# Rotary exchange by on-chip transfers and gate maxima through device memory, in a three-layer hybrid block on one core

## The reference

```python
z = rms_norm(x, w) @ w_in + b_in
aq, ak = rope(z[AQ]), rope(z[AK])          # 8 heads of 64
ya = dilated_mixture_attention(aq, ak, z[AV])
mq, mk = silu(causal_short_conv(z[MQ:MV]))
hm = mlstm_chunkwise(mq, mk, z[MV], z[MI], z[MF])   # 4 heads of 128
x = x + (sigmoid(z[GA]) * (ya @ w_proj_att) + sigmoid(z[GB]) * (yb @ w_proj_mlstm)) @ w_out
x = x + square(relu(rms_norm(x) @ w_ff1)) @ w_ff2
```

```python
t1, t2 = t[..., :8], t[..., 8:16]
concatenate([t1 * cos - t2 * sin, t2 * cos + t1 * sin, t[..., 16:]])
```

## Time and profile before

| | |
|---|---|
| median of 3 runs | 2493.03 us (2492.36 to 2494.66) |
| the profiled execution's own time | 2492.54 us |
| its span, first to last instruction | 2490.7 us |
| PE busy | 2444.8 us (98%), granted clock 0.998 on the mean |
| DVE, ACT, POOL busy | 983.9, 868.4, 1099.4 us (40%, 35%, 44%) |
| transfers | 215.18 MB, 86 GB/s on the mean |

### The profile page before, as it was taken

The page is one execution under the profiler, slowest core; times in us unless marked ns, Lnnn a source line. Parts: engine busy times, 40 slices in busy tenths (PEclk is TensorE's granted clock), DMA queues, the critical chain, the costliest instruction groups (busy, mean ns, idle before and its releaser), DMA issues.

```text
span 2490.7 us, 30039 instructions
## 1 busy us (share of the span) xinstructions
PE 2444.8 (98%) x11732; PEld 1984.8 (80%) x11732; DVE 983.9 (40%) x1582; ACT 868.4 (35%) x1092; POOL 1099.4 (44%) x808
## 2 busy tenths in 40 slices
PE   7999999999999999999999999999999999999998
PEld 6777788888888867788888888898776688888887
DVE  4545553310202455554310212567695543322202
ACT  4355333421323345333421323442325323322213
POOL 3423344544544532345454544443342255555542
PEclk9999999999999999999999999999999999999999
DMA  4211223223222221222322322321222132232231
GB/s 140 90 63 53 83 85 101 85 102 101 85 102 89 85 68 51 85 78 91 101 101 85 101 102 70 101 77 51 74 85 68 55 101 92 95 101 85 101 101 68
DMA packets 174028, 215.18 MB, mean 86 GB/s; under 512 B 7652, under 2 KB 155044, under 8 KB 173924
## 3 DMA queue, kind: packets, MB, share of 16 engines
q1 hardware_dynamic: 171572, 210.39, 26.1%
q10 hardware_dynamic: 2352, 3.31, 0.4%
HBM read 211.20 MB, written 2.10 MB: 86 GB/s over the span
## 4 chain that ended last, share of the span: by engine, by line
issue 49%; POOL 31%; PE 19%; DMA 0%; POOLq 0%; DVE 0%; ACT 0%; SPq 0%
POOL w_lo L290 31%; PE ps L329 4%; PE ps L331 4%; PE ps L330 3%; PE ps L736 3%; PE ps L1760 2%; PE ps L1758 2%; PE ps L1756 2%; DMA w_raw<-in_w_in 0%; POOLq L301 0%; PE ps L318 0%; PE ps L355 0%; PE ps L348 0%; PE ps L349 0%; PE ps L322 0%
## 5 line engine op out<-in xcount | busy, mean ns | idle before, releaser
L290 POOL TENSOR_TENSOR w_lo<-w_raw,w_hi 128x512 fp32r<-128x512 f32 x804 | 1099.2, 1399 | 1364.7 <-ACT w_hi L276 1352.5
L276 ACT ACTIVATE w_hi<-w_raw 128x2048 fp32r<-128x2048 f32 x200 | 383.0, 1915 | 1030.7 <-PE ps L331 394.1
L736 PE MATMUL ps<-h_hi,w_hi 128*128 128x512 f32 (+1 forms) x936 | 395.6, 423 | 8.2 <-POOL w_lo L290 5.1
L736 PE MATMUL ps<-h_hi,w_lo 128*128 128x512 f32 (+1 forms) x936 | 366.8, 392 | 0.0
L736 PE MATMUL ps<-h_lo,w_hi 128*128 128x512 f32 (+1 forms) x936 | 366.1, 391 | 0.0
L329 PE MATMUL ps<-h_hi,w_hi 128*128 128x512 f32 x816 | 319.0, 391 | 0.0
L331 PE MATMUL ps<-h_hi,w_lo 128*128 128x512 f32 x816 | 317.5, 389 | 0.0
L330 PE MATMUL ps<-h_lo,w_hi 128*128 128x512 f32 x816 | 317.4, 389 | 0.0
L736 PEld LDWEIGHTS ps<-h_hi,w_hi 128*128 128x128 f32 (+1 forms) x936 | 174.0, 186 | 69.8 <-issue 26.6
L736 PEld LDWEIGHTS ps<-h_lo,w_hi 128*128 128x128 f32 (+1 forms) x936 | 174.2, 186 | 44.5 <-issue 9.6
L736 PEld LDWEIGHTS ps<-h_hi,w_lo 128*128 128x128 f32 (+1 forms) x936 | 173.7, 186 | 41.2
(11 more groups left out here) (407 smaller groups left out, 3644.9 us busy)
## 6 DMA issues: line engine op xcount, KB each, us to landing
w_raw<-in_w_in SPq DMA_DIRECT2D x72, 1024.0 KB, 5.1
w_raw<-in_w_ff SPq DMA_DIRECT2D x64, 1024.0 KB, 5.2
w_raw<-in_w_ffn_in SPq DMA_DIRECT2D x22, 1024.0 KB, 5.0
w_raw<-in_w_out SPq DMA_DIRECT2D x12, 1024.0 KB, 5.1
w_raw<-in_w_ffn_out SPq DMA_DIRECT2D x11, 1024.0 KB, 4.8
w_raw<-in_w_proj_att SPq DMA_DIRECT2D x4, 1024.0 KB, 5.1
w_raw<-in_w_proj_mlstm SPq DMA_DIRECT2D x4, 1024.0 KB, 5.0
w_raw<-in_w_up_ssd SPq DMA_DIRECT2D x4, 1024.0 KB, 5.1
```

The costliest lines, as they stand in the source:

```text
L276: act.activation(k.whi[:, slot * SLOT:(slot + 1) * SLOT], k.wraw[:, slot * SLOT:(slot + 1) * SLOT], ACT.Copy).then_inc(k.hi_done, CHUNKS)
L290: pool.tensor_tensor(k.wlo[:, a:a + T], k.wraw[:, a:a + T], k.whi[:, a:a + T], ALU.subtract)\
L736: mm = pe.matmul(out, lhs, rhs, start=i == 0 and n == 0, stop=stop and n == 2)
```

## The change

The exchanged rows are no longer made by a product. `rope_swapped` (8 tiles of 128x512, where attention's output will lie) is cleared once a layer by DVE. When ACT has applied the bias to the second tile of a query or key unit, it waits for its own result and issues four transfers from qk to `rope_swapped`, each of 8 rows of 1024 values (`move`): rows 8 to 15 and 0 to 7 of both heads. The sign now sits in the table of frequencies (its first half is negative), so sin carries it. Rope has no PE work of its own; DVE does two tiles with one instruction, 12 instead of 24. It gets 18 pieces and attention 36, where it was 14 and 40.

Gates leaves out the clearing; ACT waits for the scan of maxima and stores the 4 rows to a small array in device memory. A new stage, Maxima, between attention and convolution on ACT, reads them back to all 128 partitions (1 MB). Mlstm loses its four products and copies, and 4 of its 32 steps, with 60 pieces as before. The angles' scratch moves to make room.

```diff
-BESIDE1 = {"turn": 2, "forget": 5, "gates": 9, "rope": 14, "att": 40, "conv": 12, "mlstm": 60}
+BESIDE1 = {"turn": 2, "forget": 5, "gates": 9, "rope": 18, "att": 36, "conv": 12, "mlstm": 60}
...
+                if job.move:
+                    eng.wait_ge(*self.posted(job))
+                    job.move(eng)
...
+    def move(self, j):
+        half, w = ROPE_DIM // 2, slice(2 * j * T, (2 * j + 2) * T)
+
+        def issue(act):
+            for h in (0, HD):
+                act.dma_start(self.swapped[h:h + half, w], self.qk[h + half:h + 2 * half, w])\
+                   .then_inc(self.sem("swapped"), 16)
+                act.dma_start(self.swapped[h + half:h + 2 * half, w], self.qk[h:h + half, w])\
+                   .then_inc(self.sem("swapped"), 16)
+        return issue
...
     def pe(self, pe):
-            pe.matmul(k.ps[:, 4 + t % 4, :], k.const(C_ROT), self.qk[:, t * T:(t + 1) * T],
-                      start=True, stop=True).then_inc(self.sem("swapped"), 1)
-            self.side_pe(pe, t, 8)
+        self.side_pe(pe, 0, 1)
...
+        for j in range(self.UNITS):
+            self.side_out("dve", dve, j, self.UNITS)
...
+            if j == 0:
+                dve.wait_ge(*self.at("swapped", 64 * self.UNITS))
+            dve.scalar_tensor_tensor(tiles, tiles, scale, both(k.cos[:, :]), ALU.mult, ALU.mult)\
                .then_inc(self.sem("cos"), 1)
+            dve.scalar_tensor_tensor(swapped, swapped, scale, both(k.sin[:, :]), ALU.mult, ALU.mult)\
                .then_inc(self.sem("sin"), 1)
...
+            dve.tensor_tensor(tiles, tiles, swapped, ALU.add).then_inc(self.sem("turned"), 1)
+        self.side_out("dve", dve, 1, 1)
...
 class Gates, def act
+        act.wait_ge(*self.at("scan", 4))
+        act.dma_start(self.rows.rearrange("a (h t) -> (a h) t", t=T), k.gm[0:MH, :]).then_inc(self.sem("kept"), 16)
         self.side_out("act", act, 1, 2)
...
 class Mlstm, def pe
-            pe.matmul(k.ps[:, 4 + h, :], k.pick(h), k.gm[:, :], start=True, stop=True)\
-              .then_inc(self.sem("spread"), 1)
...
 class Mlstm, def act
-            act.activation(self.mb[:, h * T:(h + 1) * T], k.ps[:, 4 + h, :], ACT.Copy)\
-               .then_inc(self.sem("maxima"), 1)
...
+class Maxima(Stage):
+    def act(self, act):
+        self.join(act)
+        act.wait_ge(*self.gates.at("kept", 16))
+        act.dma_start(self.mb[:, :], self.gates.rows.broadcast_to([P, MH * T])).then_inc(self.sem("landed"), 16)
...
+        dve.memset(self.swapped, 0.0)
```

More of the change, by code:

```diff
@@ L83 @@
 C_ID, C_ONE = 0, P
-C_ROT, C_QK, C_ST, C_KEEP, C_PAT = (P + 8 + P * i for i in range(5))
+C_QK, C_ST, C_KEEP, C_PAT = (P + 8 + P * i for i in range(4))
 C_INV = C_PAT + TT * P
@@ L99, in constants @@
     c[:, C_ONE:C_ONE + 8] = 1.0
[L100 to L106, removed]
     c[:, C_QK:C_QK + P] = np.where(i[None, :] > i[:, None], BIG, 0.0)
@@ L115, in constants @@
     inv = np.float32(ROPE_THETA) ** (-np.arange(0, ROPE_DIM, 2, dtype=np.float32) / np.float32(ROPE_DIM))
-    c[:, C_INV] = np.where(d < ROPE_DIM, inv[d % half], 0.0)
+    half = ROPE_DIM // 2
+    c[:, C_INV] = np.where(d < ROPE_DIM, np.where(d < half, -inv[d % half], inv[d % half]), 0.0)
     c[:, C_MSK] = d < ROPE_DIM
@@ L596, with __init__ @@
 class Job:
-    def __init__(self, who, evac, c=None, tm=None, need=(), rows=P, post=None):
+    def __init__(self, who, evac, c=None, tm=None, need=(), rows=P, post=None, move=None):
         self.who, self.evac, self.c, self.tm, self.need, self.rows, self.post = who, evac, c, tm, need, rows, post
+        self.move = move
 class Jobs(Stage):
@@ L774, with __init__ @@
 class Rope(Stage):
-    def __init__(self, k, name, prev, qk, t1, t2, gates):
+    UNITS = 4
+    def __init__(self, k, name, prev, qk, swapped):
         super().__init__(k, name, prev)
-        self.qk, self.t1, self.t2, self.gates = qk, t1, t2, gates
-        self.ends = [self.at("turned", 8)]
+        self.qk, self.swapped = qk, swapped
+        self.ends = [self.at("turned", self.UNITS)]
     def tally(self):
-        return {"cos": 8, "swapped": 8, "sin": 8, "turned": 8}
-    def pe(self, pe):
[L787 to L793, removed]
-            pe.matmul(k.ps[:, 4 + t % 4, :], k.const(C_ROT), self.qk[:, t * T:(t + 1) * T],
-                      start=True, stop=True).then_inc(self.sem("swapped"), 1)
-            self.side_pe(pe, t, 8)
+        return {"swapped": 64 * self.UNITS, "cos": self.UNITS, "sin": self.UNITS, "turned": self.UNITS}
+    def move(self, j):
[7 more added lines that the diff above has]
+        return issue
+    def pe(self, pe):
+        self.side_pe(pe, 0, 1)
     def dve(self, dve):
@@ L1209, in pe @@
         for h in range(MH):
-            pe.matmul(k.ps[:, 4 + h, :], k.pick(h), k.gm[:, :], start=True, stop=True)\
-              .then_inc(self.sem("spread"), 1)
-            self.side_pe(pe, step, self.steps)
-            step += 1
-        for h in range(MH):
-            if h == 0:
-                pe.wait_ge(*self.at("maxima", MH))
             pe.wait_ge(*self.conv.at("silu", MH + h + 1))
@@ L1280, in dve @@
             if h == 0:
-                self.side_out("dve", dve, self.AHEAD, self.steps)
-                dve.wait_ge(*self.at("maxima", MH))
+                self.side_out("dve", dve, 0, self.steps)
+                for end, value in self.maxima.ends:
+                    dve.wait_ge(end, value)
             else:
@@ L1969, in __init__ @@
         self.positions, self.table = positions, table
-        self.posi = k.at("setup_positions", at, T, I32)
-        self.w = [k.at(f"setup_w{i}", at + (i + 1) * T, T) for i in range(4)]
+        self.posi = k.at("setup_positions", at[0], T, I32)
+        self.w = [k.at(f"setup_w{i}", a, T) for i, a in enumerate(at[1:])]
         self.ends = [self.at("step", 16)]
@@ L2738, in scaled, with biased @@
         return Job("dve", evac, c=c % UT, post=post)
-    def biased(dst, c, bcol):
-        return scaled(dst, c, lambda act: act.activation(dst, dst, ACT.Identity, bias=k.col(c0 + bcol)))
+    def biased(dst, c, bcol, move=None):
+        job = scaled(dst, c, lambda act: act.activation(dst, dst, ACT.Identity, bias=k.col(c0 + bcol)))
+        job.move = move
+        return job
     def att_values(j, half):
@@ L3120, in program @@
         k.stream_sems()
+        k.maxima = nc.dram_tensor("maxima", (DEPTH, MH * T), F32, kind="Internal").ap()
         st = []
```

92 lines of the change are left out of this document (47 added, 45 removed).

## The result

| | before | changed |
|---|---|---|
| median, timed side by side | 2493.85 us (2492.36 to 2496.08) | 2479.07 us (2478.76 to 2479.43) |
| ratio, 95% interval | | 0.994 (0.9927 to 0.9952) |
| span of the profiled execution | 2490.7 us | 2477.5 us |
| PE busy, granted clock | 2444.8 us, 0.998 | 2425.7 us, 0.999 |

The account below looks back on a forecast made before the run. PE, busy 2444.8 of 2490.7 us, was taken to bound the kernel. Products -20.9, rotation waits +1.0 and attention +1.0 gave -18.9 us: 2493.0 to 2474.1 us, range 2469 to 2483.

Parts of the forecast that it names:

- Products, 20.9 us: 24 products taken off PE, in the rotation and for the maxima, at 0.87 us each: 20.9 us less.
- Rotation, 0.5 a layer: In the rotation, new waits of PE on DVE and POOL together: 0.5 us a layer, 1.0 in all.
- Rival (a): POOL becomes the wait in the rotation, 2.6 instead of 0.5 us a layer, and can drop the clock: 2481.7 us; chance 0.12.
- Attention, 0.5 a layer: Dealing 36 pieces over attention's 57 steps adds 0.5 us a layer, 1.0 in all; bounds 0 and 5.5.
- Transfers on ACT: Four issues of exchanged rows take at most 1.6 us on ACT before a rounding; cost nothing, or some tenths.
- Maxima's read: Its 0.4 us issue delays ACT's convolution, but a 0.71 us step left that path: net nothing, -0.7 to +0.5 a layer.
- mLSTM's start: Third score's weighting ready near 245.4, PE there at 246.0: holds by 0.6 us, else at most a microsecond a layer.
- Store, landing and clearing: ACT's store of the maxima, the transfers' landing and DVE's clearing all stay hidden: no cost.
- (b): Attention does not get shorter by its four pieces: 2484 us; chance 0.08.
- (c): More than the products go, as an earlier rounding in the convolution ends the lower clock: 2470.5 us; chance 0.08.
- (d): Attention's waits grow until the lower clock is granted there, each stream product 0.2 us more: 2560 us; chance 0.03.
- (e): The transfers do not come in time, so the rotation starts late: about 2493 us; chance 0.03.

Follow-up runs that it names:

- the rotation alone: Changed kernel's new rotation and shares, but the maxima still made by their 8 products on PE: median 2480.44 us, ratio 0.9949 to the kernel before.
- the narrow run: Changed kernel with the rotation on DVE as 24 instructions of 512 elements a partition in place of 12 of 1024: span 2485.8 us.
- the run with 39 pieces: Against the fastest run: 39, 16, 53 pieces beside attention, convolution, mLSTM for 36, 16, 56, one more rounding ahead of a SiLU pair: 2487.32 us.
- the maxima alone: Maxima's rows through device memory, but the rotation by its 16 products with 14 and 40 pieces: median 2491.35 us, ratio 0.999 to the kernel before.

## Why the prediction was right, and where not

It said 2474.1 us, 2469 to 2483; the measured 2479.07 lies inside, 5 us above the point. The cause is the one given, products off PE with losses around them. The losses were set at 2.0 us and are 7.7, so the point was missed by the losses alone.

- **Products, 20.9 us.** No product of the rotation or of the maxima is left. The price holds where it can be read again (13.1 us for four products and seven pieces). That the rotation alone gained 13.1 of 13.9 us does not show it, as 2.9 of them came from the convolution. In the end the maxima's 7.0 are worth 1.3, because both their neighbours turned into waits.
- **Rotation, 0.5 a layer.** Waits on POOL of 0.55 and 0.57 us, none on DVE: right as a wait, though the stage lost 0.8. "First score 1.5 to 2.5 us earlier" was wrong: from the transposes it came 0.7 us earlier (40.82 to 40.10), of 1.5 that products and pieces give. POOL's windows were set at 7.5 and took 7.97 and 9.05: the step that scaled 0.35 us a chunk with the length of DVE's steps was too low. A window is a first chunk of 1.29 to 2.35 us here, and 2.3 for each of the other three. The exclusive lock of the Trainium skill (SBUF — State Buffer, section "SBUF: two separate sides"), which I priced at 9.7 us, comes near to the second window, and the narrow run agrees in kind (6.60 us beside steps of 0.68, 7.97 to 9.05 beside steps of 1.22), if not in full: taking strict turns, four chunks beside narrow steps would be 7.7. Rival (a) named the right mechanism, but its wait of 2.6 us did not come: the longer window is the second, and PE waits for the first.
- **Attention, 0.5 a layer.** It was 1.0, of which 0.7 are a new wait for ACT at the last values: the term was too small by half, and the run with 39 pieces shows that it can't be read from a number of pieces.
- **Transfers on ACT, "nothing, or some tenths".** This step failed. Their issues were priced at 0.41 us from a transfer out of device memory; these took 0.63 to 0.65, the first 1.25, and the rounding came 3.5 us later instead of 1.8. The cover ran out at 57.26: 1.2 us in an execution with the upper clock there. That the issues of the other moves cost nothing was right (0.3 us at most with all of them left out).
- **Maxima's read, "net nothing, -0.7 to +0.5".** The changed kernel has +0.3 and -0.2. Both parts were there, and the read's was larger: the missing `mo` step took 0.7 off the wait, the read put 1.0 on it (2.21 to 3.19 alone), 0.5 by its issue and 0.5 by POOL's first chunk, which the prediction did not count. Landing 4.4 us, within 3.1 to 12.4, hidden.
- **mLSTM's start, "holds by 0.6 us, else at most a microsecond".** In layer 2 it failed by 1.58, 2.3 us in the stage. The largest miss: the step took PE's arrival from the first layer, with the lower clock behind it, and layer 2 kept the upper one, before (23.99 us from the last values to the mLSTM, 25.58 in layer 1) as after (wait 1.98, then 0.39 products), so PE came 1.6 us sooner than the step had it. The run without the transfers bears it out in layer 1: with the upper clock there PE waits 0.94 us at the same place.
- **Store, landing and clearing at nothing.** Right: the store of 0.31 us at 89.72 moved a rounding from 86.07 to 90.15, no wait follows; the clearing of 3.47 us ended 0.26 us before it was needed.
- **PE's list of waits** was to grow by 1 to 3 us and grew by some 6.
- **Rivals (b) to (e)** did not come. The mechanism of (c) did in the half change: with the rotation alone the clock behind the convolution's wait stayed up.

## To carry to other kernels

A product taken off a full TensorE is worth its price only as far as the next engine's work keeps arriving: go through every engine's next due time in each stage, at the upper clock, and move the side work with it (here 4 pieces and the places of one rounding and one issue were worth another 7 us). Price an issue by a row with the same kind of source and destination. Before comparing spans that differ by a few microseconds, find a point in the trace behind the parts whose clock differs from run to run, and count from there.

## What was not expected of the hardware

- ACT's queue needs 0.63 to 0.65 us to issue a transfer of 8 rows of 4 KB inside the on-chip memory (the first 1.25), 0.36 for 1 MB from device memory, 0.31 for 8 KB to it.
- A DVE step with two on-chip inputs is held by up to 1.1 us beside POOL's split whatever its width (0.68 to 1.78, 1.22 to 2.31), one step for each chunk. POOL's chunk, 1.25 us alone, takes 1.7 beside steps of 512 and 2.3 beside steps of 1024. Only a window's first chunk differs, from 1.29 to 3.07 us in these traces, with the point at which it meets DVE's row of steps, and so the same four chunks beside 512-wide taps took 6.42, 6.91 or 8.15 us.
- After waits of PE in the convolution of nearly the same length the granted clock was the lower or the upper one. Before, 2.21 us: lower in layer 1 (0.63 us), upper in layer 2. Changed, 2.56 us: lower; with the transfers left out, 2.54 us: upper. With the maxima alone, 3.19 us: upper in layer 1, and 3.17 us: lower in layer 2. With the first issues later, 2.54 and 1.98 us: upper for five and four products, then lower to the mLSTM's start. After 0.9 to 1.6 us it stayed the upper one each time. So such a wait is priced as itself, and as itself and 1 to 2 us. In the changed kernel the clock made 0.4 us at most, as PE waits for DVE next.
- The wait at 45 us goes the same way: in the four profiles where it was 3.30 to 3.58 us the lower clock was there at once, and where it was 2.91 to 3.03 us it came in two of ten, after six products. Whether the longer wait brings the clock or both have one cause is not shown.
